# Folding the final combine into the expert blocks of a mixture-of-experts layer, with all low-weight differences on GpSimd

## The chip, the cores and the metric

One NeuronCore of a Trainium2 chip runs the whole program. The metric is the device time of one execution in microseconds. A profile is one further execution, taken by the hardware profiler. Engines are named as in the profile: PE (TensorE), DVE (VectorE), ACT (ScalarE), POOL (GpSimd), SP (SyncE).

## The reference

One layer over 2048 tokens of width 1024: a norm and a gated linear recurrence (left out here), then a mixture of 16 experts in 4 groups. A token goes to the best group and to the two best experts of that group; its output is the residual stream x plus g2 times the two experts' weighted outputs, normed. All is float32.

```python
def grouped_moe(h, router_w, router_b, w_gate, w_up, w_down):
    ...
    top_w = top_vals / jnp.sum(top_vals, axis=-1, keepdims=True)
    gates = jnp.sum(jax.nn.one_hot(top_idx, N_EXPERTS, dtype=jnp.float32) * top_w[..., None], axis=-2)
    g = jnp.einsum('bsd,edf->bsef', h, w_gate)
    u = jnp.einsum('bsd,edf->bsef', h, w_up)
    act = jax.nn.silu(g) * u * gates.astype(g.dtype)[..., None]
    out = jnp.einsum('bsef,efd->bsd', act, w_down)
...
        x = x + g1[:, None, :] * y
        hn = modulate(rmsnorm(x, norm2_g[i]), sh2, sc2)
        x = x + g2[:, None, :] * grouped_moe(hn, router_w, router_b, moe_w_gate[i], moe_w_up[i], moe_w_down[i])
    return rmsnorm(x, final_norm_g)
```

## The kernel before

The program is a row of stages with a barrier between them. The last four matter here.

`out_and_norm` (from L669) computes the mixer's output product and the residual stream `x2`, which stays in SBUF for all 16 tiles of 128 tokens, writes the normed hidden rows to `hn2_dram`, and computes the router's logits.

`dispatch` (from L900) picks the two experts of each token on DVE, counts, and gives each (token, choice) pair a slot. Slots come in blocks of 128 of one expert. One-hot products on PE turn this into tables for each block: `slot_token` (the token of each slot), `slot_gate` (half of its gate), `expert`, `woff` (which of two weight buffers), and `split0`, `split1` (whether a half of the next expert's weights is to be split in this block). Meanwhile the first expert's weights are loaded and split, and SP fills the slot rows that no block writes (L995).

`experts` (from L1164) runs over the blocks. Float32 products are made of three products of rounded parts: a number is split into a high part (a rounded copy, made by ACT) and a low part (the difference, `low_w`, `low_x`, `low_a`). For each block POOL gathers 128 hidden rows by index (L1226 the copy of the indices, L1229 the indirect DMA); PE transposes them, multiplies with gate and up weights (L1377 to 1379), transposes the activation and multiplies with the down weights (L1400 to 1402); DVE scales the result with gate and g2 (`y_scaled`, L1327), and ACT's queue stores it in `yslot_dram`. The expert's weights come in four quarters of 128x1536 through two raw buffers: SP loads a quarter when the low part of the one before it in that buffer is done, ACT rounds it (L1272), and `low_w` (L1214) takes the difference: even quarters on DVE, odd ones on POOL. An expert's first block splits quarters 0 and 1 of the next expert, its second block quarters 2 and 3; an expert with one block does both. The order within an engine is written by hand: a loop over blocks in which stages of neighbouring blocks follow one another. Each engine takes its instructions in order.

`combine` (from L1422) runs after a barrier over the 16 tiles: POOL gathers each token's two slot rows (L1446, L1451), DVE adds them and x2 (L1483, L1485), ACT squares and takes the root (L1473, L1475), DVE inverts and scales (L1489, L1493), SP stores.

## Time and profile before

| | before |
|---|---|
| median of 3 runs | 1336.73 us (1335.91 to 1336.91) |
| the profiled execution's own time | 1335.74 us |
| its span | 1334.2 us |
| mean granted TensorE clock | 0.926 |
| busy PE / DVE / ACT / POOL | 1082.2 / 769.5 / 567.3 / 563.5 us |
| indirect DMAs' queue (q0) | 54.01 MB |

The span reaches from the first to the last instruction. The granted clock is a share of full speed. The recurrence and its projections take the first 560 us, `out_and_norm` ends at about 772, `dispatch` at 827, `experts` at 1255, and `combine` ends the span.

### The profile page before, as it was taken

To read this page: it belongs to the slowest core of one execution; us is meant where nothing else is said; L and a number is where in the kernel's file an instruction comes from. 1 tells how busy PE (TensorE), PEld (TensorE's weight loads), DVE (VectorE), ACT (ScalarE), POOL (GpSimd) and SP (SyncE) were. 2 spreads that over 40 slices of the span, in tenths; PEclk is the share of its full clock that TensorE was granted. 3 is DMA by queue.
4 is the path that set the end of the run, shared out by engine and by line. 5 is a ranking of instruction groups with operands and counts; after the bars stand their busy time and mean duration, and the time that the engine had idled before them with its cause. 6 is when DMAs were issued, how large, how long until landed. Compare 5 with 4: busy or idle time off the path is not lost. (4 is left out here: it accounts for less than half of the span.)

```text
span 1334.2 us, 19676 instructions
## 1 busy us (share of the span) xinstructions
PE 1082.2 (81%) x4894; PEld 866.6 (65%) x4895; DVE 769.5 (58%) x874; ACT 567.3 (43%) x792; POOL 563.5 (42%) x394
## 2 busy tenths in 40 slices
PE   1459999999999994899999814899999999989300
PEld 0247778778778773688888714677777776767200
DVE  6984676667667664545343376354544545445288
ACT  1554666766776673422222220333433334334033
POOL 0686625525526420145455243333433333334273
PEclk9999999999999997899999855999999999999755
DMA  8544314313313201833324144466756567667498
GB/s 303 175 89 151 99 33 130 84 46 114 93 53 114 63 16 38 311 126 98 139 94 141 48 142 174 135 210 209 262 199 228 189 211 241 206 207 236 145 350 324
DMA packets 126572, 207.59 MB, mean 156 GB/s; under 512 B 16961, under 2 KB 84545, under 8 KB 126417
## 3 DMA queue, kind: packets, MB, share of 16 engines
q1 hardware_dynamic: 106096, 132.81, 30.7%
q0 software_dynamic: 14832, 54.01, 12.0%
q10 hardware_dynamic: 5616, 20.45, 3.8%
q8 instruction: 12, 0.20, 0.1%
q14 instruction: 16, 0.12, 0.0%
HBM read 156.36 MB, written 50.87 MB: 155 GB/s over the span
## 5 line engine op out<-in xcount | busy, mean ns | idle before, releaser
L1214 POOL TENSOR_TENSOR w_lo<-w_raw,w_hi 128x1536 f32 x30 | 107.1, 3570 | 157.8 <-ACT w_hi L1272 157.8
L1377 PE MATMUL e_gu<-w_hi,e_xh 128*128 x312 | 130.2, 417 | 13.7 <-issue 5.0
L1272 ACT ACTIVATE w_hi<-w_raw 128x1536 f32 x60 | 88.3, 1486 | 121.1 <-PE e_pd L1402 46.3
L849 PE MATMUL po<-wo_hi,b_yh 128*128 128x512 f32 x256 | 102.9, 402 | 25.6 <-DVE wo_lo L779 25.6
L1379 PE MATMUL e_gu<-w_hi,e_xl 128*128 x312 | 123.5, 396 | 0.0
L1378 PE MATMUL e_gu<-w_lo,e_xh 128*128 x312 | 122.8, 394 | 0.0
L823 POOL TENSOR_TENSOR x<-x,b_xr 128x1024 f32 (+1 forms) x15 | 49.1, 3273 | 171.9 <-DVE x L787 171.9
L531 DVE SCALAR_TENSOR_TENSOR XB<-xu,conv_w,XB 128x512 f32<-128x512 f32 x96 | 92.6, 965 | 42.2 <-ACT XB L401 38.5
L624 PE MATMUL px<-hT_hi,wx_hi 128*128 128x512 f32 x256 | 101.7, 397 | 5.1 <-DVE wx_lo L465 5.1
L624 PE MATMUL pg<-hT_hi,wg_hi 128*128 128x512 f32 x256 | 104.2, 407 | 0.0
L625 PE MATMUL px<-hT_lo,wx_hi 128*128 128x512 f32 x256 | 101.6, 397 | 0.0
L626 PE MATMUL px<-hT_hi,wx_lo 128*128 128x512 f32 x256 | 101.4, 396 | 0.0
L626 PE MATMUL pg<-hT_hi,wg_lo 128*128 128x512 f32 x256 | 101.1, 395 | 0.0
L625 PE MATMUL pg<-hT_lo,wg_hi 128*128 128x512 f32 x256 | 101.1, 395 | 0.0
L850 PE MATMUL po<-wo_lo,b_yh 128*128 128x512 f32 x256 | 100.4, 392 | 0.0
L851 PE MATMUL po<-wo_hi,b_yl 128*128 128x512 f32 x256 | 100.4, 392 | 0.0
L1327 DVE SCALAR_TENSOR_TENSOR e_y<-e_pd,t_slot_gate,g2row 128x1024 f32<-128x1024 f32 x39 | 50.1, 1284 | 66.2 <-DMA yslot_scratch<-e_y 37.8
L606 POOL TENSOR_TENSOR macc<-macc,mtmp 128x512 f32<-128x512 f32 x56 | 84.4, 1507 | 4.7
L1377 PEld LDWEIGHTS e_gu<-w_hi,e_xh 128*128 128x128 f32 x312 | 59.3, 190 | 39.7 <-issue 29.9
L787 DVE TENSOR_TENSOR x<-po,g1row 128x1024 f32 (+1 forms) x16 | 19.6, 1224 | 108.7 <-PE po L851 108.7
L600 POOL TENSOR_SCALAR macc<-stg,cond 128x512 f32<-128x512 f32 x8 | 12.1, 1512 | 155.2 <-PE pmod L647 151.3
L1400 PE MATMUL e_pd<-w_hi,e_ah 128*128 x156 | 64.8, 415 | 12.1 <-issue 6.5
(260 smaller groups left out, 2639.4 us busy)
## 6 DMA issues: line engine op xcount, KB each, us to landing
yslot_scratch<-e_y ACTq DMA_DIRECT2D x39, 512.0 KB
stg<-in_ada_w_dram POOLq DMA_DIRECT2D x32, 512.0 KB, 4.2
w_raw<-in_moe_w_gate_dram SPq DMA_DIRECT2D x32, 384.0 KB, 3.3
w_raw<-in_moe_w_up_dram SPq DMA_DIRECT2D x32, 384.0 KB, 4.0
n_ada<-in_ada_w_dram SPq DMA_DIRECT2D x16, 512.0 KB, 4.8
n_x<-in_x_dram SPq DMA_DIRECT2D x16, 512.0 KB, 3.4
y_scratch<-M SPq DMA_DIRECT2D x16, 512.0 KB, 3.0
b_yt<-y_scratch SPq DMA_DIRECT2D x16, 512.0 KB, 5.3
```

The costliest lines, as they stand in the source:

```text
L531: nc.vector.scalar_tensor_tensor(xb, xu[:, n, w:w + NB], cw[:, ds(j, 1), w], xb, ALU.mult, ALU.add).then_inc(done, 1)
L624: nc.tensor.matmul(dst[:], whi[br][:, k], hT_hi[:, k, cols], start=(k == 0), stop=False)
L625: nc.tensor.matmul(dst[:], whi[br][:, k], hT_lo[:, k, cols], start=False, stop=False)
L626: last = nc.tensor.matmul(dst[:], wlo[br][:, k], hT_hi[:, k, cols], start=False, stop=(k == KD - 1))
L849: nc.tensor.matmul(po[u][:, cols], yh[u][:, tok], wo_hi[:, k, cols], start=(k == 0), stop=False)
L850: nc.tensor.matmul(po[u][:, cols], yh[u][:, tok], wo_lo[:, k, cols], start=False, stop=False)
L851: last = nc.tensor.matmul(po[u][:, cols], yl[u][:, tok], wo_hi[:, k, cols], start=False, stop=(k == KD - 1))
L1214: tensor_tensor(w["lo"][:, ds(off + q * QW, QW)], w["raw"][:, q % 2], w["hi"][:, ds(off + q * QW, QW)].bitcast(F32), ALU.subtract).then_in ...
L1272: nc.scalar.activation(w["hi"][:, ds(off + q * QW, QW)], w["raw"][:, q % 2], ACT.Copy).then_inc(w["hi_done"], 1)
L1377: nc.tensor.matmul(gu[:], xh[:, tok], hi, start=(k == 0), stop=False)
L1378: nc.tensor.matmul(gu[:], xh[:, tok], lo, start=False, stop=False)
L1379: last = nc.tensor.matmul(gu[:], xl[:, tok], hi, start=False, stop=(k == KD - 1))
```

## The change

- `out_and_norm` also stores every tile of x2 to DRAM (`store_x2`, in SP's queue between its load and its store); x2 is no longer kept.
- `dispatch` numbers the experts in another order (`expert_at`), in which two experts of a group are four places apart. It writes no slot rows. The token code of a slot carries whether it is the token's first or second slot; from it come three index tables: `row` (the token of a slot, out of bounds where it is empty), `row_first` (in bounds only for a token's first slot) and `row_second` (only for its second).
- `experts` gathers the residual rows of a block from `x2_dram` (`gather_x`), adds the block's scaled outputs to them on DVE (`accumulate`), scatters the sums back for first slots (`scatter_acc`), and takes square (ACT), reciprocal root (POOL, a power and one Newton step) and norm (DVE, `normed`) of all rows, of which those of second slots are final and are scattered to the output (`scatter_out`). Rows out of bounds are skipped by the DMA. The gate is now multiplied into the activation.
- `low_w` of all four quarters runs on POOL.
- `combine` is gone.

```diff
+            def store_x2(it, u):
+                sp.wait_ge(resid, it + 1)
...
+                sp.dma_start(x2_dram[ds(it * P, P), :], x2[:, ds(it, 1)].rearrange("p o n -> p (o n)"))\
+                    .then_inc(x2_stored[u], 16)
...
-            pipelined(sp, NT, 6, [(load, 0), (store, 4)])
+            pipelined(sp, NT, 6, [(load, 0), (store_x2, 3), (store, 4)])
...
+def expert_at(i):
+
+    return i % G * PER + i // G
...
-            with sp.Fori(used, MAXB + 1) as b:
-                sp.dma_start(yslot_dram[ds(b * P, P), :], g2row[:]).then_inc(filled, 16)
...
-            done(v.tensor_copy(tab["slot_token"][:], pslot[:, 0:MAXB]))
+            done(v.tensor_copy(sci[:], pslot[:, 0:MAXB]))
+            done(v.tensor_scalar(skip1[:], sci[:], float(SECOND), None, ALU.is_gt))
+            done(v.scalar_tensor_tensor(sci[:], skip1[:], -float(SECOND), sci[:], ALU.mult, ALU.add))
...
+            done(v.tensor_copy(tab["row_second"][:], skip1[:]))
...
-                    q = 2 * part + odd
-                    eng.wait_ge(w["hi_done"], NQ * e + (q + 1))
...
+                    for odd in range(2):
+                        q = 2 * part + odd
+                        eng.wait_ge(w["hi_done"], NQ * e + (q + 1))
...
+            def gather_x(b, first=False):
+                if not first:
+                    pool.wait_ge(xa_in, b * 16)
+                    pool.wait_ge(acc_ready, b)
+                pool.nop(nofuse=True)
+                nc.gpsimd.tensor_copy(idx_x[:], tab["row"][:, ds(b, 1)]).then_inc(idx_x_ready, 1)
+                pool.wait_ge(idx_x_ready, b + 1)
+                pool.nop(nofuse=True)
+                pool.indirect_dma_start(xa[:], None, x2_dram, rows(idx_x), **bound).then_inc(xa_in, 16)
+
+            def scatter_acc(b, first=False):
+                if not first:
+                    pool.wait_ge(acc_out, b * 16)
...
+                pool.wait_ge(acc_ready, b + 1)
+                pool.nop(nofuse=True)
+                pool.indirect_dma_start(x2_dram, rows(idx_a), ab[:], None, **bound).then_inc(acc_out, 16)
+
+            def scatter_out(b, first=False):
+                if not first:
+                    pool.wait_ge(out_done, b * 16)
...
+                pool.wait_ge(out_ready, b + 1)
+                pool.nop(nofuse=True)
+                pool.indirect_dma_start(out[0], rows(idx_o), ob[:], None, **bound).then_inc(out_done, 16)
+
+            def root(b, first=False):
+
+                pool.wait_ge(squared, b + 1)
+                pool.nop(nofuse=True)
+                nc.gpsimd.tensor_scalar(var[:], ssq[:], 1.0 / D, EPS, ALU.mult, ALU.add).then_inc(rstd_step, 1)
...
+                nc.gpsimd.tensor_tensor(root0[:], var[:], nhalf[:], ALU.pow).then_inc(rstd_step, 1)
...
+                nc.gpsimd.tensor_scalar(rstd[:], part[:], 1.5, root0[:], ALU.add, ALU.mult).then_inc(rstd_ready, 1)
+
+            nc.gpsimd.memset(xg[:], 0.0).then_inc(cleared, 1)
+            nc.gpsimd.memset(xa[:], 0.0).then_inc(cleared, 1)
...
+            with pool.Fori(3, nless) as i:
                 gather(i + LEAD)
-                low_w(pool, nc.gpsimd.tensor_tensor, i + 1, 1)
...
+                low_w(pool, nc.gpsimd.tensor_tensor, i + 1)
+                scatter_acc(i - 1)
+                gather_x(i)
+                root(i - 1)
+                scatter_out(i - 2)
...
+            def accumulate(b, first=False):
+                dve.wait_ge(y_ready, b + 1)
+                dve.wait_ge(xa_in, (b + 1) * 16)
+                if not first:
+                    dve.wait_ge(squared, b)
+                    dve.wait_ge(out_ready, b)
+                    dve.wait_ge(acc_out, b * 16)
+                nc.vector.tensor_tensor(ab[:], ysb[:], xa[:], ALU.add).then_inc(acc_ready, 1)
+
+            def normed(b, first=False):
+                dve.wait_ge(rstd_ready, b + 1)
+                if first:
+                    dve.wait_ge(fg_in, 16)
+                else:
+                    dve.wait_ge(out_done, b * 16)
+                dve.nop(nofuse=True)
+                nc.vector.scalar_tensor_tensor(ob[:], ab[:], rstd[:], fg[:], ALU.mult, ALU.mult).then_inc(out_ready, 1)
...
+            with dve.Fori(2, nless) as i:
                 low_a(i + 1)
                 act_product(i + 2)
                 low_x(i + 3)
-                dues = [per_block(dve, f"split{part}", i + 2, 0, 1) for part in range(2)]
+                normed(i - 1)
+                accumulate(i)
                 y_scaled(i + 1)
-                low_w(dve, nc.vector.tensor_tensor, i + 2, 0, dues)
```

On POOL, ahead of the loop over blocks, before the change: a gather is a copy of the indices (`e_idx`) and a DMA, and behind the gathers stands one difference for each part that is due (`w_lo`). TENSOR_LOAD reads a number of a table; ISA rows are waits and register work.

```order
L1226 COPY e_idx<-t_slot_token 128x1 [waits e_turned]
L1229 DMA e_xg<-hn_scratch,e_idx 128x1024 [waits idx_ready]
L1192 TENSOR_LOAD t_split
L1192 ISA x2
L1208 COMPARE_AND_BRANCH
L1192 TENSOR_LOAD t_expert
L1192 ISA x2
L1192 TENSOR_LOAD t_woff_next
L1192 ISA x2
L1212 ISA
L1214 ISA [waits w_hi_done]
L1214 TENSOR_TENSOR w_lo<-w_raw,w_hi 128x1536
```

The kernel of the change, the same engine, what now follows the differences of a block, in the loop as here: sums scattered (`e_ab`), residual rows gathered (`e_xa`), the root (`e_var` to `e_rstd`), results scattered (`e_ob`).

```order
L1285 COPY e_idx_a<-t_row_first 128x1 [waits acc_out]
L1289 DMA x_scratch<-e_ab,e_idx_a 2048x1024 [waits idx_a_ready,acc_ready]
L1276 COPY e_idx_x<-t_row 128x1 [waits xa_in,acc_ready]
L1279 DMA e_xa<-x_scratch,e_idx_x 128x1024 [waits idx_x_ready]
L1305 TENSOR_SCALAR e_var<-e_ssq 128x1 [waits e_squared]
L1308 TENSOR_TENSOR e_root<-e_var,e_nhalf 128x1 [waits e_rstd_step]
L1310 TENSOR_TENSOR e_part<-e_root 128x1 [waits e_rstd_step]
L1313 TENSOR_SCALAR e_part<-e_part,e_var 128x1 [waits e_rstd_step]
L1319 TENSOR_SCALAR e_rstd<-e_part,e_root 128x1 [waits e_rstd_step,out_ready]
L1295 COPY e_idx_o<-t_row_second 128x1
L1299 DMA out_dram<-e_ob,e_idx_o 2048x1024 [waits idx_o_ready,out_ready]
```

Nothing of this stood on POOL before; of the second difference that each due part has now, the diff shows the loop over `odd`.

On DVE, a block ahead of the loop, before: the low part of the activation, the activation, the low part of the hidden rows, the scaled output. The difference of weights follows it.

```order
L1321 TENSOR_TENSOR e_al<-e_pa,e_ah 128x256 [waits ah_ready]
L1308 SCALAR_TENSOR_TENSOR e_th<-e_th,e_gu 128x256 [waits th_ready]
L1310 TENSOR_TENSOR e_av<-e_th,e_gu 128x256 [waits tmp_ready]
L1316 TENSOR_TENSOR e_xl<-e_tp,e_xh 128x512 [waits xh_ready] x2
L1327 SCALAR_TENSOR_TENSOR e_y<-e_pd,t_slot_gate,g2row 128x1024 [waits d_mm]
```

And now, up to the head of the loop: `normed` (`e_ob`) and `accumulate` (`e_ab`) stand between the low part of the hidden rows and the scaled output.

```order
L1452 SCALAR_TENSOR_TENSOR e_av<-e_th,t_slot_gate,e_gu 128x256 [waits tmp_ready]
L1459 TENSOR_TENSOR e_xl<-e_tp,e_xh 128x512 [waits xh_ready] x2
L1488 SCALAR_TENSOR_TENSOR e_ob<-e_ab,e_rstd,e_fg 128x1024 [waits e_rstd,fg_in]
L1479 TENSOR_TENSOR e_ab<-e_y,e_xa 128x1024 [waits out_ready,e_squared,acc_out,xa_in,ey_ready]
L1470 TENSOR_TENSOR e_y<-e_pd,g2row 128x1024 [waits acc_ready,d_mm]
```

The difference of weights is gone from DVE, and the scaled output has moved behind two operations that wait for POOL and for DMAs.

## Rows read from the trace of the kernel before

**Rows 1.** Windows: length, busy us (x instructions) by engine, clock, DMA share, GB/s.
```profile
838.00:1251.00 413.00, 383.44 (x1785) 300.36 (x1783) 198.90 (x261) 156.36 (x214) 148.90 (x104) 0.99 0.62 207
...
1256.00:1334.20 78.20, 0.00 (x0) 0.00 (x0) 59.98 (x64) 24.40 (x49) 44.81 (x47) 0.50 0.88 329
```

**Rows 2.** Waits, expert part: who waited for whom, us, times, longest.
```profile
POOL w_lo L1214 <- ACT w_hi L1272: 157.8, 30, 9.0
...
PE e_gu L1377 <- DVE w_lo L1214: 4.0, 1, 4.0
```

**Rows 3.** Timeline, POOL, third gather: start, us, instruction, [idle before].
```profile
846.12 0.96 POOL L1229 DMA_INDIRECT e_xg<-hn_scratch,e_idx  x1 [0.77 <-POOL e_idx L1226]
```

**Rows 4.** Timeline, POOL, the first tile of the combine.
```profile
1255.74 0.19 POOL L1446 COPY f_idx<-t_pos 128x2 int32<-128x2 int32 x1 [22.15 <-POOLq L1169]
1256.72 0.98 POOL L1451 DMA_INDIRECT f_ya<-yslot_scratch,f_idx  x1 [0.80 <-POOL f_idx L1446]
1258.01 0.94 POOL L1451 DMA_INDIRECT f_yb<-yslot_scratch,f_idx  x1 [0.30 <-issue]
1258.95 0.20 POOL L1446 COPY f_idx<-t_pos 128x2 int32<-128x2 int32 x1
```

**Rows 5.** Source line 1214 (low-weight difference): ns min/median/max.
```profile
L1214 DVE TENSOR_TENSOR w_lo<-w_raw,w_hi x30: 1757/1759/1761, 848.7 to 1227.2; 128x1536 f32 x30
...
L1214 POOL TENSOR_TENSOR w_lo<-w_raw,w_hi x30: 3462/3502/3787, 850.1 to 1230.1; 128x1536 f32 x30
```

**Rows 6.** Source line 1192 (table numbers), POOL's sequencer.
```profile
L1192 POOLq TENSOR_LOAD <-t_split x78: 283/292/895, 845.9 to 1233.6; - x78
```

**Rows 7.** Timeline, dispatch, DVE beside POOL's difference.
```profile
778.19 7.07 POOL L968 TENSOR_TENSOR w_lo<-w_raw,w_hi 128x1536 fp32r<-128x1536 f32 x2 [4.37 <-ACT w_hi L1007]
778.64 3.30 DVE L1054 TENSOR_SCALAR d_gq<-d_gq 128x64 f32<-128x64 f32 x1
...
781.98 3.57 DVE L1055 TENSOR_TENSOR work<-work,d_gq 128x256 f32<-128x256 f32 x1
```

**Rows 8.** Groups by line, combine: busy us, mean ns, idle before.
```profile
L1493 DVE SCALAR_TENSOR_TENSOR f_ob<-x,f_rstd,f_g 128x1024 f32<-128x1024 f32 x16 | 20.5, 1284 | 2.1 <-DVE f_rstd L1489 0.8
L1483 DVE TENSOR_TENSOR f_ya<-f_ya,f_yb 128x1024 f32<-128x1024 f32 x16 | 19.6, 1222 | 14.2 <-DMA f_yb<-yslot_scratch,f_idx 14.2
...
L1473 ACT ACTIVATE f_junk<-x 128x1024 f32 x12 | 12.3, 1028 | 31.2 <-DVE f_rstd L1489 31.2
```

**Rows 9.** Timeline, dispatch and its end, POOL, then DVE.
```profile
772.39 0.31 POOL L951 MEMSET keep<- 128x256 f32 x1
...
821.95 0.89 POOL L974 TENSOR_TENSOR place<-place,tok 128x192 f32<-128x192 f32 x1 [0.54 <-DVE place L1102]
822.91 0.51 POOL L977 TENSOR_TENSOR place<-place,d_gates 128x192 f32<-128x192 f32 x1
827.84 0.18 POOL L1226 COPY e_idx<-t_slot_token 128x1 int32<-128x1 int32 x1 [4.42 <-issue]
...
826.04 0.21 DVE L1141 CAST t_slot_token<-pslot 128x48 int32<-128x48 f32 x1 [2.35 <-PE pslot L1159]
826.28 0.21 DVE L1143 TENSOR_SCALAR t_slot_gate<-pslot 128x48 f32<-128x48 f32 x1
```

**Rows 10.** Tiles e_xg and f_ya: issue (ns min/median/max) and landing.
```profile
L1229 POOL DMA_INDIRECT e_xg<-hn_scratch,e_idx x37: 961/983/986, 846.1 to 1224.8; - x37
...
DMA to landing us min/median/max: 4.2/5.3/7.6
...
L1451 POOL DMA_INDIRECT f_ya<-yslot_scratch,f_idx x16: 959/1382/1809, 1256.7 to 1315.1; - x16
```

**Rows 11.** Window and timeline, PE around 1182 us.
```profile
1182.00:1184.00 2.00, 1.95 (x6) 1.04 (x5) 0.00 (x0) 0.00 (x0) 1.24 (x1) 0.50 0.90 288
...
1181.85 0.63 PE L1377 MATMUL e_gu<-w_hi,e_xh 128*128 x1
1182.27 0.63 PE L1378 MATMUL e_gu<-w_lo,e_xh 128*128 x1
```

More of the change, by code:

```diff
@@ L30 @@
 WE = KD * 2 * FE + FE // P * D
+SKIP = 1 << 14
+SECOND = 1 << 12
 def at_least(it, k):
@@ L1082, in _ @@
             for c, oh in enumerate((oh1, oh2)):
-                done(v.tensor_tensor(work2[:], work[:], oh, ALU.mult))
+                done(v.tensor_tensor(placed_as(work2[:]), placed_as(work[:]), at(oh), ALU.mult))
                 done(v.tensor_reduce(posf[:, c], work2[:], AX.X, ALU.add))
-            pos_i = tab["pos"][:].rearrange("p c t -> p (c t)")
+            for c in range(TOPK):
+                done(v.tensor_tensor(later[:, c], posf[:, c], posf[:, 1 - c], ALU.is_gt))
+            v.scalar_tensor_tensor(tok2[:], later[:].rearrange("p c t -> p (c t)"), float(SECOND), tok2[:],
+                                   ALU.mult, ALU.add).then_inc(code_ready, 1)
+            pos_i = pos_i_t[:]
             done(v.tensor_copy(pos_i, posf[:].rearrange("p c t -> p (c t)")))
@@ L1198, in _ @@
                 load_quarter(sp, io, w, 1, q)
-            with sp.Fori(2, E) as e:
+            sp.dma_start(fg[:], io["final_norm_g"].partition_broadcast(P)).then_inc(fg_in, 16)
+            for e in range(2, E):
                 for q in range(NQ):
@@ L1220, in _ @@
             nless = blocks_less(pool)
+            rows = lambda t: bass.IndirectOffsetOnAxis(ap=t[:], axis=0)
+            bound = dict(bounds_check=S - 1, oob_is_err=False)
             def gather(b, first=False):
@@ L1238, in _ @@
-            low_w(pool, nc.gpsimd.tensor_tensor, nless + 1, 1)
-            low_w(pool, nc.gpsimd.tensor_tensor, nless + 2, 1)
+            low_w(pool, nc.gpsimd.tensor_tensor, 0)
+            gather(3)
+            low_w(pool, nc.gpsimd.tensor_tensor, 1)
+            gather(4)
+            low_w(pool, nc.gpsimd.tensor_tensor, 2)
+            scatter_acc(0, True)
+            gather_x(1)
+            root(0, True)
+            gather(5)
+            low_w(pool, nc.gpsimd.tensor_tensor, 3)
+            scatter_acc(1)
@@ new lines, in _ @@
+            scatter_out(nless - 2)
+            low_w(pool, nc.gpsimd.tensor_tensor, nless + 2)
+            scatter_acc(nless)
+            gather_x(nless + 1)
+            root(nless)
+            scatter_out(nless - 1)
+            scatter_acc(nless + 1)
+            gather_x(nless + 2)
+            root(nless + 1)
+            scatter_out(nless)
+            root(nless + 2)
+            scatter_out(nless + 1)
+            scatter_out(nless + 2)
+            pool.wait_ge(acc_out, (nless + 2) * 16)
@@ L1241, in _ @@
+            pool.wait_ge(out_done, (nless + LEAD) * 16)
+            pool.nop(nofuse=True)
         @block.scalar
@@ L1273, in high_w, with square @@
                                                  ACT.Copy).then_inc(w["hi_done"], 1)
-            def store(b):
-                act.wait_ge(y_ready, b + 1)
-                act.dma_start(yslot_dram[ds(b * P, P), :], ysb[:]).then_inc(y_out, 16)
+            def square(b, first=False):
+                act.wait_ge(acc_ready, b + 1)
+                if not first:
+                    act.wait_ge(rstd_ready, b)
+                act.nop(nofuse=True)
+                nc.scalar.activation(squares[:], ab[:], ACT.Square, accum_out=ssq[:]).then_inc(squared, 1)
             high_x(0)
@@ L1336, in _ @@
             y_scaled(0, True)
-            low_w(dve, nc.vector.tensor_tensor, 1, 0)
-            with dve.Fori(0, nless) as i:
+            low_a(1)
+            act_product(2)
+            low_x(3)
+            accumulate(0, True)
+            y_scaled(1)
+            low_a(2)
+            act_product(3)
+            low_x(4)
+            normed(0, True)
+            accumulate(1)
+            y_scaled(2)
+            with dve.Fori(2, nless) as i:
                 low_a(i + 1)
@@ L1541, in build @@
                  "hi_done": sem("w_hi_done"), "lo_done": [sem("w_lo_done0"), sem("w_lo_done1")]}
[L1542 to L1544 removed]
+            dispatch(nc, sem, cst, io, logits, tab, w)
+            experts(nc, sem, cst, io, tab, w, hn2_dram, x2_dram, g2row, out)
 _INS = ["x", "c", "ada_w", "ada_b", "norm1_g", "norm2_g", "lru_w_in", "lru_conv_w", "lru_conv_b", "lru_wa", "lru_ba",
```

232 lines of the change are left out of this document (110 added, 122 removed).

## The prediction

> **What bounds the kernel now.** I first read the table of windows for the last 500 us. From 838 to 1251 us, the expert blocks, PE is busy 383 of 413 us and the DMA queues carry 207 GB/s; from 1256 to 1334.2 us, the combine, PE does nothing [rows 1]. So the expert part is bound by TensorE: 39 blocks in 413 us, 10.6 us for each. The combine costs 78 us in which TensorE does nothing, and that is what the change wants to hide. Next, the list of waits: POOL's differences waited 157.8 us for ACT's rounded weights, and PE waited for a difference once, 4.0 us [rows 2]. POOL has slack, but it is all the slack there is for the new work, so the question is what POOL's own steps cost.
>
> **POOL's prices.** POOL takes its instructions in order. An indirect DMA is a copy of 128 indices, a gap of 0.77 us in which the DMA waits for that copy, and the issuing, 0.96 us in one case [rows 3] and 0.98 in the median [rows 10]; the copy is 0.19 us [rows 4], 1.94 in all. The combine, where POOL has nothing to wait for, confirms it start to start: a tile takes 1258.95 - 1255.74 = 3.21 us, of which the second DMA is 1.24, and the next copy starts the moment that DMA ends [rows 4]. A low-weight difference takes 3.5 us on POOL against 1.76 on DVE [rows 5]. POOL's sequencer loads a number of the table in 0.29 us [rows 6]; the two "is it due" numbers go by under the DMA before them, and a due part adds two more, with the register work on them about 0.8 us.
>
> **The lock.** In dispatch, DVE's subtraction on 128x64 takes 3.30 us and the next operation, on 128x256, 3.57 us, while POOL's two differences run [rows 7]; outside of them an operation on 128x48 takes 0.21 [rows 9]. DVE gets in between two POOL instructions, not beside one. In the expert blocks DVE is not held up, because its operations there have one input in PSUM. The two new ones of 128x1024 (accumulate, normed) read both inputs from SBUF, so each waits out a difference. Their prices stand in the combine: 1.22 and 1.28 us; the square is 1.03 on ACT, and I take 1.3 with reading out its sum [rows 8].
>
> **The change, part by part.**
> 1. Combine removed: 78.2 us [rows 1] and some 4 us of barrier ahead of it.
> 2. The slot-row fill in dispatch goes: SP issued it beside the one-hot products, which DVE, POOL and PE work through in that time whatever SP does, so nothing.
> 3. Dispatch gets 11 DVE steps of 128x48 after the last matmul, plus a net one ahead. Two such steps start 0.24 us apart [rows 9]: 12 x 0.24 = 2.9 us, all on the path, since POOL's first copy waits for the barrier behind them.
> 4. The expert part opens with two memsets of 128x1024. One of 128x256 takes 0.31 us [rows 9], so at most 1.24 each; part of the 0.31 is a fixed cost, I take 1.0 each and 2.1 with the wait. Start of POOL's first gather: 827.8 + 2.9 + 2.1 = 833.
> 5. The store of x2 (16 x 0.5 MB) lies under TensorE's work in the stage before; nothing. If that cover went, only the last store, about 3 us, could show.
> 6. DVE loses 30 differences of 1.76 us and gains 39 x 2.5; it has room and is no bound.
> 7. POOL, each block: four copies with a DMA in place of one (hidden states, residual rows, sums out, results out): 7.8 us. The reciprocal root adds five dependent operations on 128x1. The tightest pair of dependent POOL operations in the trace has 0.07 us between them [rows 9]; a DMA behind its copy has 0.80 and one without a dependence 0.30, so 0.5 is the most that a wait written apart adds [rows 4]. Five operations at 0.19 with 0.07 to 0.5 between: 1.3 to 3.4 us. No row shows a power on POOL; I take 1.9. Without weights a block is 9.7 us of POOL. All differences: 60 x 3.57 = 214 us in place of 107.
>
> **The round.** From the code, result b can't be computed (normed waits on out_done) before the scatter of result b-1 has landed, and that scatter is issued only after root(b). DVE is in order, so accumulate(b+1) stands behind normed(b), and POOL's scatter of the sums b+1 waits for accumulate(b+1). Landings of the gathers of hidden rows take 4.2 to 7.6 us, median 5.3 [rows 10]; a scatter moves about half of the rows, I take 5.0. From the end R of root(b):
> - No weights due: scatter issued from R+1.0, landed 6.0, normed 7.3, accumulate 8.6, scatter of sums 9.6, gather of residuals 11.5, root 13.4. Round: **13.4 us**.
> - One part due (two differences): they start at R+4.7; normed, ready at 6.0, is locked out until 8.2 and ends at 9.5; the second difference ends at 13.0, accumulate at 14.3, then 1.0 + 1.9 + 1.9. Round: **19.1 us**.
> - Both parts due (an expert with one block; one such): the third quarter must be loaded and rounded between, about 3 us of wait, plus 7 + 1: 30 us.
>
> TensorE's 10.6 us fits in any of these. It will idle several us a block and its clock will drop as at 1182 us, where, behind that wait of 4.0 us [rows 2], it was granted 0.50, the lower level of 1.2 GHz, and matmuls came 0.42 us apart [rows 11]. A block of 36 such matmuls and 10 transposes is then 18 us at worst, still under a round with weights.
>
> **The sum.** The routing of these inputs gives 16 experts 39 blocks; in the new order 3,3,3,1,2,2,2,2,3,3,3,2,2,3,3,2. The last expert splits nothing, so 28 blocks have one part due, one has two, 10 none. The ramp: the third gather ended at 847.1 us before [rows 3], 19.3 after POOL's first copy, plus 8.6 for the first two differences, then eight indirect steps (15.6), root twice (3.8) and two due parts with a wait for a load (17.8): 65 us. The loop, 33 rounds: 25 x 19.1 + 7 x 13.4 + 30.1 = 601. Three rounds without weights: 40. From the last-but-one root: normed 7.3, accumulate 8.6, square 9.9, root 11.8, scatter, landed 17.8, normed 19.1, last scatter landed 24. The span: 833 + 65 + 601 + 40 + 24 = 1563 us. The profiled execution took 1335.74 us for a span of 1334.2, so 1.5 more: **1565 us**. Its own time is within 0.1% of the median of 1336.73, and I compare directly. About 230 us slower.
>
> **Two rules of the Trainium skill against rows.** In the combine the same DMA issue took 0.96 to 1.81 us, median 1.38, under DVE operations with two SBUF inputs [rows 10]. The Trainium skill ("SBUF — State Buffer", the section "Who interferes with whom") says that such an operation takes only the read side of the port and that writing descriptors needs the write side (inferred there), so that they don't collide; by it nothing is added, by the row 0.4 us for each of the four DMAs in the worst case. I add nothing in the middle, since DVE's two operations rarely lie over an issue here, and keep 0.4 for the upper end. For the landing the row says 5.3. The Trainium skill ("DMA: Bandwidth & Descriptors", the section "Anatomy of one DMA — SWDGE (gpsimd) path") fits 2.0 us plus the bytes over 436 GB/s, 2.6 us for 256 KB; by that estimate the ten rounds without weights shrink by 2.4 us each and the sum by some 30 us. The row is a transfer of this kernel, so I keep it.
>
> **Rivals.**
> - A, the forecast (0.60): POOL's chain with the landing and the lock in it, 1565.
> - B (0.20): landing and lock hide, POOL's own occupancy bounds: 9.7 and 17.6 us a round. 25 x 17.6 + 7 x 9.7 + 28.6 = 537, three rounds 29: 833 + 65 + 537 + 29 + 24 + 1.5 = 1489. For it: each wait has other work beside it. Against: the order just read.
> - C (0.14): small operations and issues are dear: root at 3.4 and 0.4 more for each DMA make a round 2.9 longer, 36 x 2.9 = 104: 1669. A power far above a copy's cost leads here too.
> - D (0.05), faster: TensorE stays the bound, the combine disappears. Its end moves 5 us later to 1256, then about 13 us of tail (add, square, root, norm, scatter, landing): 1271. It decides at 10.6 us of POOL a block; break-even is at a mean round of (1334.2 - 833 - 65 - 24) / 36 = 11.5 us. With 1.9 for the root and 5.5 for the differences, an indirect step would have to cost 1.0 us, not 1.95. Scatters that skip half their rows may be cheaper, gathers are not.
> - That the tail or ramp alone eats the gain and the time stays (0.01).
>
> **How the numbers follow.** A measurement of this kernel can tell some 0.2% from no change. Only D is faster: 0.05; same 0.01; slower 0.94. The range runs from B with the cheaper root (0.6 x 39 = 23 us less, 1466) to short of C's full price, of which half of its chance is left out, with D and the last case: 1460 to 1650.
>
> **What would show it.** In the profile after: POOL busy or waiting on its own indices all the time in the expert blocks; the start-to-start of hidden-row gathers near 19 us where weights are due and 13 where not; normed released by the landing of the result scatter; accumulate or normed right behind a difference; PE at half its share, granted clock under 0.9. Wrong if issues cost under 1.2 us each, if the root costs over 4, or if PE stays above 90% busy there.

## The result, and the profile after

| | before | after |
|---|---|---|
| median | 1336.32 us (1334.18 to 1336.91, 4 runs) | 1600.12 us (1598.79 to 1606.09, 4 runs) |
| span of the profiled execution | 1334.2 us | 1597.2 us |
| mean granted TensorE clock | 0.926 | 0.861 |
| busy PE / DVE / ACT / POOL | 1082.2 / 769.5 / 567.3 / 563.5 us | 1151.1 / 775.8 / 582.4 / 830.4 us |

The change makes the kernel 264 us slower: a ratio of 1.199 (95% interval 1.195 to 1.202).

The windows of the changed kernel, which answer to [rows 1]: the expert part, then its tail (length, busy us by PE, PE's weight loads, DVE, ACT and POOL, clock, DMA share, GB/s).

```profile
850.00:1580.00 730.00, 449.10 (x1794) 353.72 (x1794) 259.92 (x311) 196.40 (x292) 471.05 (x555) 0.79 0.41 131
1580.00:1597.20 17.20, 0.00 (x0) 0.00 (x0) 1.57 (x2) 1.15 (x2) 4.89 (x9) 0.50 0.09 37
```

PE was busy 383 of 413 us and is now busy 449 of 730, at a granted clock of 0.79. The stretch without TensorE has shrunk from 78 us to a tail, as the change meant. What it paid stands in POOL's column, and in what is not busy there. The timeline of POOL over one round with a part due (start us, busy us, instruction, idle before and its releaser):

```profile
1106.19 0.19 POOL L1266 COPY e_idx<-t_row 128x1 int32 x1
1107.33 1.05 POOL L1269 DMA_INDIRECT e_xg<-hn_scratch,e_idx  x1 [0.95 <-POOL e_idx L1266]
1109.41 7.90 POOL L1251 TENSOR_TENSOR w_lo<-w_raw,w_hi 128x1536 f32 x2 [1.03 <-issue]
1117.26 0.18 POOL L1285 COPY e_idx_a<-t_row_first 128x1 int32 x1
1118.36 1.07 POOL L1289 DMA_INDIRECT x_scratch<-e_ab,e_idx_a  x1 [0.92 <-POOL e_idx_a L1285]
1119.44 0.19 POOL L1276 COPY e_idx_x<-t_row 128x1 int32 x1
1120.51 1.05 POOL L1279 DMA_INDIRECT e_xa<-x_scratch,e_idx_x  x1 [0.87 <-POOL e_idx_x L1276]
1121.63 0.19 POOL L1305 TENSOR_SCALAR e_var<-e_ssq 128x1 f32<-128x1 f32 x1
1121.98 0.57 POOL L1308 TENSOR_TENSOR e_root<-e_var,e_nhalf 128x1 f32<-128x1 f32 x1 [0.16 <-POOL e_var L1305]
...
1123.51 0.27 POOL L1319 TENSOR_SCALAR e_rstd<-e_part,e_root 128x1 f32<-128x1 f32 x1 [0.24 <-POOL e_part L1313]
1123.72 0.18 POOL L1295 COPY e_idx_o<-t_row_second 128x1 int32 x1
1124.82 1.10 POOL L1299 DMA_INDIRECT out_dram<-e_ob,e_idx_o  x1 [0.92 <-POOL e_idx_o L1295]
1125.93 0.19 POOL L1266 COPY e_idx<-t_row 128x1 int32 x1
```

The round is 1125.93 - 1106.19 = 19.74 us, forecast as 19.1. But no idle time in it is a wait for another engine or for a landing: each gap is POOL's own, a copy before its DMA or "issue" (nothing that the profile shows). A step of copy and DMA takes 2.2 us (1119.44 to the root's start at 1121.63 is 2.19), four of them 8.7, the root 2.15, the two differences 7.9, and 1.0 lies ahead of them. That sums to the round. A round without weights, from the same view, with the sum's copy in it:

```profile
936.34 0.19 POOL L1266 COPY e_idx<-t_row 128x1 int32 x1
...
939.20 1.11 POOL L1285 COPY e_idx_a<-t_row_first 128x1 int32 x1 [0.65 <-issue]
...
948.74 0.19 POOL L1266 COPY e_idx<-t_row 128x1 int32 x1
```

It takes 12.40 us, forecast as 13.4; another of the loop's seven such rounds takes the same, the other five 12.8 to 13.6, of which more below. DVE's view of the first stretch shows the other side:

```profile
1108.35 1.28 DVE L1488 SCALAR_TENSOR_TENSOR e_ob<-e_ab,e_rstd,e_fg 128x1024 f32<-128x1024 f32 x1 [8.02 <-DMA out_dram<-e_ob,e_idx_o]
1109.85 4.14 DVE L1479 TENSOR_TENSOR e_ab<-e_y,e_xa 128x1024 f32<-128x1024 f32 x1 [0.22 <-DVE e_ob L1488]
```

normed does wait for the landing of the scatter, and accumulate is stretched from 1.23 to 4.14 us by the difference beside it, as forecast. But both are done at 1114, three microseconds before POOL asks for the sums. In all 26 rounds with differences in them the sums are ready 4.4 us or more before their scatter is issued. A wait of 8 us on an engine that nobody is waiting for costs nothing. The list of waits gives the totals (us, times, longest), and the last row is the landing of the result scatters (us min/median/max):

```profile
DVE e_ob L1488 <- DMA out_dram<-e_ob,e_idx_o: 357.0, 38, 13.5
...
PE e_tp L1534 <- DMA e_xg<-hn_scratch,e_idx: 161.2, 27, 12.5
...
PE e_pa L1560 <- POOL w_lo L1251: 61.8, 7, 11.8
...
DMA to landing us min/median/max: 2.2/3.0/3.5
```

The largest wait of the trace, 357 us, is the one that the forecast built its round on: a ring of result scatter, landing, `normed`, `accumulate`, scatter of the sums, residual gather and root. It is not what sets the 26 rounds with weights; the experiments below test this.

Where no difference is due, POOL does wait for DVE. That is so in five of the loop's seven rounds without weights (the first row, from its last round, is one) and in the three rounds behind the loop, which have no gather either (POOL's timeline):

```profile
1526.91 1.04 POOL L1289 DMA_INDIRECT x_scratch<-e_ab,e_idx_a  x1 [2.29 <-DVE e_ab L1479]
...
1540.64 0.98 POOL L1289 DMA_INDIRECT x_scratch<-e_ab,e_idx_a  x1 [5.39 <-issue]
...
1554.10 0.97 POOL L1289 DMA_INDIRECT x_scratch<-e_ab,e_idx_a  x1 [5.39 <-DVE e_ab L1479]
...
1567.52 0.97 POOL L1289 DMA_INDIRECT x_scratch<-e_ab,e_idx_a  x1 [5.77 <-DVE e_ab L1479]
```

The last three are 13.4 us apart, the forecast's ring in the open. In the loop's five rounds `normed` starts 2.8 to 3.5 us after the issue of the result scatter that it waits for; in the two rounds of 12.4 us it starts after 2.3, and POOL waits for nothing. So without weights the ring and POOL's own work are nearly level: the ring adds 5 us in the whole loop.

### The profile page after: what moved, and what is told of

Its sections match the earlier page's. It is cut to its first block and busy times, and to the rows that moved or that the text cites. A ratio compares the mean times of both kernels' runs of the same rounds, so it can differ in the third digit from the quotient of the medians.

```text
span 1597.2 us, 20092 instructions
## 1 busy us (share of the span) xinstructions
PE 1151.1 (72%) x4894; PEld 921.3 (58%) x4895; DVE 775.8 (49%) x869; ACT 582.4 (36%) x821; POOL 830.4 (52%) x806
## 3 DMA queue, kind: packets, MB, share of 16 engines
q0 software_dynamic: 26928, 67.15, 13.4%
## 5 line engine op out<-in xcount | busy, mean ns | idle before, releaser
L1251 POOL TENSOR_TENSOR w_lo<-w_raw,w_hi 128x1536 f32 x60 | 223.4, 3742 | 44.4 <-issue 34.1
L1488 DVE SCALAR_TENSOR_TENSOR e_ob<-e_ab,e_rstd,e_fg 128x1024 f32<-128x1024 f32 x39 | 50.1, 1284 | 357.0 <-DMA out_dram<-e_ob,e_idx_o 357.0
L1534 PE MATMUL e_tp<-ident,e_xg 128*128 128x128 f32 x312 | 62.9, 368 | 161.2 <-DMA e_xg<-hn_scratch,e_idx 161.2
L1410 ACT ACTIVATE e_sq<-e_ab 128x1024 f32<-128x1024 f32 x39 | 41.3, 1058 | 330.4 <-DVE e_ab L1479 330.4
L1534 PEld LDWEIGHTS e_tp<-ident,e_xg 128*128 128x128 f32 x312 | 51.9, 192 | 175.0 <-DMA e_xg<-hn_scratch,e_idx 172.7
L1553 PE MATMUL e_gu<-w_lo,e_xh 128*128 x312 | 126.5, 406 | 0.0
L533 DVE SCALAR_TENSOR_TENSOR XB<-xu,conv_w,XB 128x512 f32<-128x512 f32 x96 | 92.4, 963 | 42.5 <-ACT XB L403 38.8
L1575 PE MATMUL e_pd<-w_hi,e_ah 128*128 x156 | 81.5, 522 | 34.8 <-DVE e_al L1464 31.0
```

The lines of the kernel that those rows point to most:

```text
L533: nc.vector.scalar_tensor_tensor(xb, xu[:, n, w:w + NB], cw[:, ds(j, 1), w], xb, ALU.mult, ALU.add).then_inc(done, 1)
L1251: tensor_tensor(w["lo"][:, ds(off + q * QW, QW)], w["raw"][:, q % 2], w["hi"][:, ds(off + q * QW, QW)].bitcast(F32), ALU.subtract).then_in ...
L1534: last = nc.tensor.transpose(tp[:, k * P:(k + 1) * P], xg[:, k * P:(k + 1) * P], cst["ident"][:])
L1553: nc.tensor.matmul(gu[:], xh[:, tok], lo, start=False, stop=False)
```

## The experiments

The second column of this table is a measure that leaves out everything ahead of the expert part and its tail: the issue of the first gather of hidden rows to that of the 39th, over 38 rounds. The third is the mean of such a round, with and without weights due.

| kernel | first to last gather, us | a round | median, us | ratio to before (95% interval) |
|---|---|---|---|---|
| before | 395.9 | 10.4 | 1336.32 | 1 |
| after | 672.4 | 17.7 | 1600.12 | 1.199 (1.195 to 1.202) |
| out_early | 688.4 | 18.1 | 1592.50 | 1.191 (1.187 to 1.195) |
| root_dve | 608.2 | 16.0 | 1519.45 | 1.137 (1.134 to 1.141) |
| copies_early | 614.4 | 16.2 | 1539.99 | 1.154 (1.151 to 1.157) |
| low_dve | 634.3 | 16.7 | 1558.71 | 1.165 (1.160 to 1.170) |
| low_out | 637.8 | 16.8 | 1541.33 | 1.154 (1.150 to 1.158) |
| all_dve | 549.6 | 14.5 | 1478.76 | 1.109 (1.105 to 1.113) |
| best1 | 608.8 | 16.0 | 1513.89 | 1.134 (1.130 to 1.137) |
| best2 | 466.0 | 12.3 | 1369.81 | 1.027 (1.024 to 1.031) |
| best3 | 497.8 | 13.1 | 1404.98 | 1.051 (1.047 to 1.055) |
| best4 | 455.3 | 12.0 | 1358.10 | 1.017 (1.015 to 1.020) |
| before_x2 | 394.1 | 10.4 | 1346.09 | 1.008 (1.006 to 1.010) |
| before_x2_free | 391.7 | 10.3 | 1344.90 | 1.007 (1.004 to 1.010) |

### Is the round a ring or POOL's occupancy?

**out_early** takes the landing out of the forecast's ring.

```diff
             with pool.Fori(3, nless) as i:
                 gather(i + LEAD)
                 low_w(pool, nc.gpsimd.tensor_tensor, i + 1)
+                scatter_out(i - 2)
                 scatter_acc(i - 1)
                 gather_x(i)
                 root(i - 1)
-                scatter_out(i - 2)
```

> In each round the scatter of the normed rows goes ahead of the scatter of the sums instead of behind the root. Theory of the ring (the prediction's): the round waits for that scatter's landing; issued some 6 us earlier it has landed before the root is ready, and what is left is POOL's own work: 13.4 us shrinks to about 9.7 and 19.1 to 17.6, so 7 x 3.6 + 25 x 1.5 in the loop and 3 x 3.6 behind it, about 70 us less, 1530 us. Theory of occupancy (POOL is bound by its own instructions, as the changed kernel's trace suggests): the loop has the same instructions and stays at 12.4 and 19.8 us a round; only the three rounds behind the loop, in which the trace shows POOL waiting 5.4 to 5.8 us each for the accumulate, lose about 3 us each: 1590 us.

Measured: 1592.5 us, 7.6 less. The loop got longer, not shorter (688 against 672 us from gather to gather); what lies behind the last gather fell from 75.2 to 56.6 us, the three rounds in it from 13.4 to 10.2 each. In the profiled execution (1598.4 us, the slowest of its four) the two cancel. In the loop DVE's wait for the landing is nearly gone (one of 9.8 us is left), and it buys nothing: normed now falls on the next gather instead of on the differences, and the median issue of a gather is 1.43 us in place of 1.05, the copy ahead of it 1.26 in place of 0.19 where they meet. The rounds without weights take 12.7 us each, 0.4 less than before in the mean; those with one part due 19.9 to 20.7 but for one of 22.6. The ring does not set the loop's rounds with weights.

**root_dve** takes the root off POOL, **copies_early** only its gaps.

```diff
-            def root(b, first=False):
...
             def normed(b, first=False):
+                dve.wait_ge(squared, b + 1)
+                step(lambda: nc.vector.tensor_scalar(var[:], ssq[:], 1.0 / D, EPS, ALU.mult, ALU.add))
+                step(lambda: nc.vector.tensor_scalar(root0[:].bitcast(I32), var[:].bitcast(I32), -0.5, 1597463007.0,
...
```

> The reciprocal root leaves POOL (five operations on 128x1) and is computed by DVE ahead of the normed product: an integer start value and three Newton steps, 11 operations on 128x1. Theory of occupancy: POOL loses 2.1 to 2.3 us in each of 39 blocks, about 85 us less, 1515 us; DVE's 11 operations, 0.24 us each or 2.6 us a block, find room. Theory of the ring: the root stands in the ring wherever it is computed, 2.6 us in place of 1.9, so no gain: 1600 to 1625 us.

Measured: 1519.45 us, 81 less, where occupancy (POOL's instructions and the gaps between them) said 85 and the ring nothing.

```diff
-                gather(i + LEAD)
+                copy_h(i + LEAD)
+                copy_a(i - 1)
+                copy_x(i)
+                send_h(i + LEAD)
                 low_w(pool, nc.gpsimd.tensor_tensor, i + 1)
-                scatter_acc(i - 1)
-                gather_x(i)
+                send_a(i - 1)
+                copy_o(i - 2)
+                send_x(i)
                 root(i - 1)
-                scatter_out(i - 2)
+                send_o(i - 2)
```

> The index copies of the loop's rounds are issued well ahead of their DMAs, with other work between, so no DMA stands directly behind the copy that it needs. Nothing is added or left out. Theory of occupancy: a step of copy and DMA, 2.2 us in the changed kernel with 0.9 of gap between the two, loses some 0.5 us for each of four: 2 us in each of 33 rounds, about 65 us less, 1535 us. Theory of the ring: only what stands between landing and root gets shorter, the gaps of the residual gather and of nothing else that counts, about 0.5 us a round: 1583 us. If the gap is the DMA's own start and not a wait for the copy, nothing changes: 1600 us.

Measured: 1540.0 us, 60 less, 58 of it from gather to gather: 1.5 us a round, with the same instructions. In its trace, sums and residual rows are issued with 0.16 us ahead of them, where the changed kernel has 0.92 and 0.87; gathers and result scatters keep 0.73 and 0.58. Most of the gap of [rows 3] is a wait for the copy, and other work fills it. The two edits leave the ring nearly as it was and shorten the loop by 64 and 58 us, about as POOL's occupancy, gaps included, said. In the rounds with weights, occupancy sets the time.

### What the differences cost on either engine

**low_dve** gives DVE the even quarters back, as in the kernel before.

> The differences of the even quarters go back to DVE as in the kernel before; all else is the changed kernel. It undoes one of the change's two parts. Theory of occupancy: POOL loses 30 differences of 3.45 to 3.95 us, 29 of them in rounds that it bounds: about 107 us less, 1493 us. Theory of the ring: in a round with a part due only one difference stands ahead of the sums' scatter, the round falls from 19.1 to about 15.5, 25 x 3.6 + ramp 7 = 97 us less: 1503 us. A third theory, that DVE with its stretched operations is as full as POOL: under 50 us less, over 1550 us.

Measured: 1558.7 us, only 41 less; of the three stated sizes only the third theory's (under 50) fits, and that theory was not shown. Its trace, POOL in one round with a part due:

```profile
1111.29 1.10 POOL L1298 DMA_INDIRECT out_dram<-e_ob,e_idx_o  x1 [0.91 <-POOL e_idx_o L1294]
...
1116.79 3.42 POOL L1250 TENSOR_TENSOR w_lo<-w_raw,w_hi 128x1536 f32 x1 [2.29 <-ACT w_hi L1401]
1120.16 1.18 POOL L1284 COPY e_idx_a<-t_row_first 128x1 int32 x1
1122.26 1.06 POOL L1288 DMA_INDIRECT x_scratch<-e_ab,e_idx_a  x1 [0.92 <-POOL e_idx_a L1284]
```

POOL now waits for ACT's weights (46.6 us in all, 10.2 in the changed kernel), DVE's accumulate lasts 4.45 us beside POOL's difference, and the small copy behind it 1.18 in place of 0.18. From 846 us on, POOL's differences take 113.2 us in place of 223.4, but this copy takes 42.5 in place of 10.4, and all of POOL's instructions together 411.7 in place of 478.4: of 110 us saved 67 are left, and the longer waits take part of those. **low_out** adds out_early's edit to it, to see whether the ring has taken over.

> The kernel low_dve (even quarters' differences on DVE, which came out at 1559 us where occupancy alone gave 1493) with the scatter of the normed rows ahead of the scatter of the sums, as in out_early, where that edit alone changed nothing. Theory that the prediction's ring takes over once POOL is relieved (root, scatter, landing 2.9 us, normed, accumulate under the lock, scatter of sums, root; 18.0 us from root to root in low_dve's trace): the landing drops out, rounds with a part due fall to about 16: 1495 us. Theory that the shortfall comes from the weights' loads, released late by DVE: the order of the scatters does not matter but for the last three rounds: 1550 us.

Measured: 1541.3 us, 17 less, nearer to the second theory's 1550 than to 1495, and neither. The gather-to-gather stretch did not shorten (637.8), so the gain lies behind the loop. DVE waits for the landing once in place of 38 times, but its difference is now the locked one (median 4.28 us, 2.31 in low_dve). The lock has taken the landing's place; what sets these rounds is not shown further.

**all_dve** leaves POOL no difference at all.

```diff
-                low_w(pool, nc.gpsimd.tensor_tensor, i + 1)
...
                 y_scaled(i + 1)
+                low_w(dve, nc.vector.tensor_tensor, i + 2, (0, 1), dues)
```

> All 60 differences on DVE and none on POOL, the opposite of what the change does to them; all else is the changed kernel. Theory that the two together cost what they do because POOL and DVE lock each other out (a difference takes 3.4 to 4.4 us on POOL, and one on DVE beside it 4.0 instead of 1.76): no operation is left that needs the lock for long, and POOL's round is four steps of 2.2, the root 2.1 and some 0.5, 11.3 to 12.4 us, with the ring of scatter, landing, normed, accumulate, scatter, gather and root at 12.5 to 13: 848 + 55 + 36 x 12.8 + 22, about 1386 us. Theory that the low-weight work costs its engine time wherever it stands: DVE takes over 60 x 1.76 us in series with accumulate and normed, rounds of 15 to 16 us: 1480 us, no better than the other edits.

Measured: 1478.8 us, the second theory's number. The lock is gone from the differences: DVE's 60 take 1.75 to 1.80 us each. But a round is 14.5 us, not 12.8, and now POOL does wait for DVE in nearly all rounds (all_dve: its waits from 900 to 1330 us, then rows of POOL's timeline):

```profile
DVE e_ob L1481 <- DMA out_dram<-e_ob,e_idx_o: 120.8, 28, 5.9
...
POOL x_scratch L1289 <- DVE e_ab L1472: 94.9, 27, 4.7
...
1101.39 1.75 POOL L1276 COPY e_idx_x<-t_row 128x1 int32 x1
...
1117.84 1.90 POOL L1279 DMA_INDIRECT e_xa<-x_scratch,e_idx_x  x1 [0.84 <-POOL e_idx_x L1276]
```

That is the forecast's ring. DVE's differences are not in it by their own time, as the second theory had it: behind them `normed` still waits for the landing, 28 times and 4.3 us in the mean. They lengthen it from beside: the residual gather's copy and issue, and the root's first step, fall on them and take up to 1.75, 1.90 (median of all issues 1.70, in place of 1.04) and 0.74 us. **best2** breaks the ring by out_early's order, and puts three copies together.

```diff
-                gather(i + LEAD)
-                scatter_acc(i - 1)
-                gather_x(i)
-                root(i - 1)
-                scatter_out(i - 2)
+                copy_h(i + LEAD)
+                send_h(i + LEAD)
+                copy_o(i - 2)
+                copy_a(i - 1)
+                copy_x(i)
+                send_o(i - 2)
+                send_a(i - 1)
+                send_x(i)
+                root(i - 1)
```

> all_dve, and POOL's round in another order: gather of the hidden rows, the three other index copies together, then scatter of the normed rows, scatter of the sums, gather of the residual rows, root. POOL 8.9 us a round, DVE (1.28 + 1.23 + 1.22 + 3.5 + 1.3 + 1.3 and gaps) about 11.4, TensorE 10.6. If DVE bounds: 848 + 50 + 36 x 11.4 + 22, about 1331 us, the kernel before's time. If TensorE does: 1302 us. If a ring through the residual rows' landing (3 to 4 us) and the weights' loads remains, 13 to 14 us a round: 1400 us.

Measured: 1369.8 us, 109 less than all_dve, and 84 of it from gather to gather; none of the three sizes. The copy edit gave 60 in copies_early. If it is worth no more here, the order that was worth 8 us while POOL was full is worth some 50 once POOL has room; that is an estimate, as the two edits were not run apart here.

### Does a relieved POOL beat the kernel before?

**best1** was a first try, with everything at once: even differences and root on DVE, copies at the head of the round, scatter first.

> All four edits together: even differences and root on DVE, index copies early, scatter of the normed rows first. POOL is left with about 11 us in a round with a part due and 6 in one without; TensorE wants 10.6; DVE has 11 to 13 with its root (2.7) and the lock. By that, rounds of 13 and 10.6 us: 848 + 55 + 26 x 13 + 7 x 10.6 + 33 + 22, about 1370 us. If the lock stretches each of DVE's two-SBUF operations by a whole difference, rounds of 16 and 1450 us. If TensorE is the bound again, 10.6 us throughout, 1310 us, faster than the kernel before.

Measured: 1513.9 us, far off all three sizes and 6 us from root_dve, which has one of the edits alone. The list of waits (900 to 1430 us) shows where it goes:

```profile
POOL e_idx_a L1265 <- DMA x_scratch<-e_ab,e_idx_a: 76.4, 24, 5.5
POOL e_idx_x L1265 <- DMA e_xa<-x_scratch,e_idx_x: 50.3, 31, 4.2
```

With the root gone, the copies at the head of the round overwrite indices of DMAs issued only just before, and wait for their landings. A copy moved ahead carries its own wait with it. **best3** and **best4** go on from best2.

```diff
-                copy_h(i + LEAD)
                 send_h(i + LEAD)
                 copy_o(i - 2)
                 copy_a(i - 1)
-                copy_x(i)
                 send_o(i - 2)
+                copy_x(i)
                 send_a(i - 1)
                 send_x(i)
+                copy_h(i + LEAD + 1)
                 root(i - 1)
```

> best2 with POOL's last gaps filled: the index copy for the next gather of hidden rows stands ahead of the root instead of right ahead of its DMA (0.9 us of gap and 0.3 of issue in best2's trace), and the residual rows' copy behind the scatter of the normed rows, so that it no longer waits 1.5 us for the landing of the gather before. If POOL's occupancy still sets the round (11.4 to 12.3 us in best2), each of 33 rounds loses 1.1 us: 1335 us, the kernel before's time. If the lock (issues of 2.4 us beside DVE's differences instead of 1.0) or TensorE sets it by now, less than half comes through: 1350 to 1370 us.

Measured: 1405.0 us, 35 slower than best2, where a gain or nothing was expected. The same mistake again: the copy ahead of the root waits until PE has turned (transposed) the rows of the gather before, and all of POOL behind it (list of waits, 900 to 1330 us; in best2 the same wait is 2.4 us there):

```profile
POOL e_idx L1266 <- PE e_tp L1558: 48.4, 12, 9.7
```

> best3 with the root off POOL altogether: ACT takes the square root behind its square, with a table load of 1.28 us ahead of it and another behind it (their price in the first stages of the trace), and DVE one reciprocal on 128x1. POOL is left with some 7 us a round, ACT gains 2.8 where it is a third busy, DVE 0.5. If POOL was the bound, TensorE or DVE is next, 10.6 to 11.2 us a round: 1310 to 1325 us, faster than the kernel before. If DVE or the weights' loads already bound best3, no gain or a loss of a few us from ACT's longer turn: as best3.

Measured: 1358.1 us (ACT takes `ACT.Sqrt` behind its square, DVE a reciprocal). That is the fastest of the changed kernels, 47 us less than best3 and 242 less than the change, but 1.7% slower than the kernel before, where 1310 to 1325 us was expected if POOL had been the bound. From 900 to 1330 us POOL now waits for DVE's `normed` 32 times, 106.5 us, so its own work no longer sets the round; its issues beside DVE's differences take up to 2.6 us. No version here beats the kernel before.

### The store of x2

> The kernel before with one thing added: the store of x2, 16 x 0.5 MB from SyncE in the stage with the output projection, which nothing reads. The prediction put it at nothing: 1336 us. The changed kernel's trace shows this stage ending some 11 us later, in which PE is no longer busy throughout and ACT waits longer for its loads: by that theory 1347 us.

> As before_x2, but SyncE no longer waits, ahead of each store of x2, for the one two tiles earlier to land; it only waits for all at the stage's end. If the cost of the store is SyncE being held up in front of its loads, it goes: 1336 us. If it is the traffic itself, queued ahead of the loads or slowing them, it stays: 1347 us, as before_x2.

Measured: 1346.1 and 1344.9 us against 1335.4 for the kernel before, measured beside them: 10.7 and 9.5 us slower, and the two not to be told apart. SyncE's wait for the store two tiles earlier costs nothing; the stores themselves do. Windows 680 to 760 us of the kernel before, then of before_x2 (columns as above):

```profile
680.00:720.00 40.00, 40.00 (x214) 34.03 (x213) 17.76 (x15) 9.63 (x14) 20.21 (x6) 1.00 0.35 118
720.00:760.00 40.00, 37.44 (x203) 32.72 (x202) 17.02 (x18) 9.96 (x17) 14.87 (x5) 0.93 0.19 72
```

```profile
680.00:720.00 40.00, 39.49 (x207) 32.95 (x206) 15.31 (x15) 10.08 (x15) 17.91 (x6) 0.98 0.44 157
720.00:760.00 40.00, 39.44 (x200) 33.03 (x198) 10.86 (x10) 8.13 (x13) 17.07 (x6) 0.97 0.38 144
```

PE, never idle in the first window before, now is a little in each (in the second, the kernel before nears the end of the stage). Over the stage (from its first add on POOL to dispatch's first instruction, 218.5 us before and 226.1 with the store) its idle time rises from 5.6 to 9.5 us and its busy time from 212.9 to 216.6, at a granted clock of 0.95 for 0.96. Ahead of it, ACT's waits for loads go up from 9.7 to 15.7 us and for the landing of the normed rows' stores from 114.0 to 124.3 (548 to 785 us); the loads of `b_yt` land in 6.0 us for 5.3 and take SyncE 0.87 us to issue for 0.34 (medians, 560 to 760 us). That loads and stores are held up by the new stores on the same queues is the likely way; no run here moved the stores to other queues. The first gather comes 9.1 us later (836.9 against 827.8), 1.4 of it from before the stage; nothing behind it got slower.

## Why the prediction was right, and where it was not

The sign, the size and the range held: 1565 forecast, 1600 measured, 2% off. Its reasons held less well, and part of the closeness is luck. The sum shows where (from the profiled executions):

| | forecast | measured |
|---|---|---|
| first gather | 833 | 848.5 |
| ramp to the loop | 65 | 68.1 |
| loop, 33 rounds | 601 | 617.8 |
| three rounds without gathers | 40 | 40.9 |
| tail | 24 | 21.9 |

- **Step 1** held: the combine and its barrier are gone. **Step 2** held: dispatch, from its first instruction on POOL to the last product there, takes 52.1 us for 51.3. **Step 3**: from the last product on POOL in dispatch to the first instruction of the expert part 6.9 us against 4.4, so 2.5 for 2.9. **Step 4**: the memsets take 0.95 us each, against 1.0.
- **Step 5 failed.** "The store of x2 lies under TensorE's work in the stage before; nothing." It costs 10.7 us by before_x2. A busy PE was no cover for this traffic. Another 4.6 us of the late start lie ahead of that stage and are no part of the change: the stage's first add on POOL starts between 553.6 and 559.1 us in the traces of all these kernels (558.2 in the changed one, 553.6 in the one before).
- **Step 6** held: DVE is busy 261 of 747 us and sets no round by its work. In best4 POOL does wait for it.
- **Step 7**: an indirect step takes 2.2 us, not 1.94: issue 1.05 to 1.10 for 0.96, gap 0.87 to 0.95 for 0.77. The root takes 2.15 where I took 1.9, its power 0.57. The pair of differences takes 6.8 to 8.1 us, not 7.0 to 7.1: DVE's work beside it stretches it, which I had counted only in the other direction. "Wrong if issues cost under 1.2 us each" names the wrong quantity: issues cost 1.05 to 1.10, the whole step 2.2.
- **The round failed as a mechanism where weights are due.** "Result b can't be computed before the scatter of result b-1 has landed" is true, and it binds only where no difference is due. In rounds with weights the forecast had `normed` locked out by the first difference and `accumulate` ready only behind the second, since it took 5.0 us for the landing, from gathers [rows 10]. The result scatters land in 2.2 to 3.5 us, median 3.0: `normed` starts ahead of the differences, `accumulate` ahead of the first or beside it, and the sums are ready 4.4 us or more before POOL issues their scatter. What sets these 26 rounds is POOL's own work: four steps of 2.2, the root 2.15, the differences, and about 1 us ahead of them. Rival B had this mechanism, with prices too low: with the measured ones, 25 x 19.8 + 7 x 12.4 + 30 = 612 us, and 5 more for the five rounds in which the ring binds, against 617.8 in the trace. Rival C had the direction of the prices.
- **Without weights** the forecast's ring holds in five rounds of seven in the loop and in the three behind it: seven rounds take 91.6 us, 93.8 by the forecast. That its 13.4 us came out to the decimal behind the loop is luck: the landing there is 1.5 us shorter than the 5.0 taken, and what follows it is dearer by as much.
- **Luck.** The 25 rounds with one part due take 497 us, 477.5 by the forecast: a wait behind the second difference that does not happen (19.1 against B's 17.6) made up for much of the prices that were too low (19.9 against 17.6). Of the signs that the prediction lists, the distances between gathers and `normed` released by the landing are there and tell A from B no better than the time does; the experiments do: out_early gave 7.6 us for a forecast 70, root_dve 81 for none.
- **The lock.** "In the expert blocks DVE is not held up, because its operations there have one input in PSUM" leaves out DVE's own 30 differences, which read both inputs from SBUF and took 1757 to 1761 ns [rows 5]. They were not held up: POOL's differences started 1.3 us or more behind them; in low_out, where both fall together, DVE's take 4.28 us in the median.
- **The two rules.** For the landing, the Trainium skill's fit ("DMA: Bandwidth & Descriptors", "Anatomy of one DMA — SWDGE (gpsimd) path") gave 2.6 us as an estimate; the runs show 3.0 in the median, so it was nearer than the row of gathers that I kept. For the port, the Trainium skill ("SBUF — State Buffer", "Who interferes with whom") says that an operation with two SBUF inputs and the writing of descriptors don't collide (inferred there). The trace of best2 does not bear that out for these DMAs. POOL's timeline, then DVE's:

```profile
1104.67 1.02 POOL L1302 DMA_INDIRECT out_dram<-e_ob,e_idx_o  x1 [0.67 <-issue]
1106.00 2.54 POOL L1296 DMA_INDIRECT x_scratch<-e_ab,e_idx_a  x1 [0.30 <-issue]
```

```profile
1103.82 1.23 DVE L1486 TENSOR_TENSOR e_y<-e_pd,g2row 128x1024 f32<-128x1024 f32 x1
1105.92 3.43 DVE L1251 TENSOR_TENSOR w_lo<-w_raw,w_hi 128x1536 f32 x2 [0.87 <-ACT w_hi L1418]
```

  Beside DVE's e_y, whose one input is in PSUM, the issue takes 1.02 us; beside the difference with both inputs in SBUF, 2.54. These DMAs also read their 128 indices from SBUF; whether that or the descriptors is held up, no run here separates. It costs the changed kernel little (gathers 1.02 to 2.01 us, median 1.05), and out_early and best2 more (medians 1.43 and 1.52).

What stays open: why best4's rounds are 12.0 us and not the 10.4 of the kernel before, and which of DVE's order, ACT's table loads, the weights' loads and POOL's lengthened issues sets them; what part of best2's gain is the order of the scatters and what part the copies; and what the new order of the experts does by itself, which no run separates.

## What to carry to other kernels

The largest wait in a trace names the bound only if somebody is waiting for the engine that waits; look for the engine whose gaps are all its own, and sum its instructions with their gaps. Do it for each kind of round: here the same wait cost nothing in 26 rounds and bound in eight. Before moving small work onto GpSimd, price it there at what it costs in a row (here 2.2 us for a gather or scatter of 128 rows with its index copy, 2.15 for five operations on 128x1, 3.4 to 4.5 for a difference that DVE does in 1.76), and remember that an instruction moved ahead takes its wait along. A transfer under a busy TensorE is not free by that alone: here, with TensorE's inputs on the same queues, 16 stores of 0.5 MB cost 10 us.

## What the runs showed of the hardware

- The lock works in both directions and reaches the smallest operations: a copy on 128x1 on POOL takes 1.11 to 1.75 us in place of 0.18 when a DVE operation with two SBUF inputs is under way (changed kernel at 939.20 us, all_dve at 1101.39), an indirect DMA's issue up to 2.6 (best2, best4) in place of 1.0; on DVE, `accumulate` 4.14 in place of 1.23.
- A scatter that skips about half its rows is not cheaper to issue than a gather of all (1.10 and 1.05 us); the result scatters land earlier (median 3.0 us against 4.3 for the gathers of hidden rows), the scatters of the sums hardly (3.9).
- 0.87 to 0.95 us of an indirect DMA's step is the gap behind its index copy; with other work between, 0.16 to 0.73 is left (copies_early), 0.30 to 0.67 in best2's round above.
